# The sample part of a width-31 depthwise convolution: one product of four samples and one sum over the taps, in place of 31 taps of 64 columns

## What is computed

```
u  = glu[..., :512] * sigmoid(glu[..., 512:])
cv = causal_dwconv(conv_hist, u, w_dw)          # width 31, each channel by itself
cv = silu(layer_norm(cv + b_dw, ln_conv_g, ln_conv_b))
br_a = cv @ w_conv_out
```

## Time and profile before

| | |
|---|---|
| time, median of 3 runs | 1377.58 us (1369.18 to 1380.51) |
| profiled execution, first to last instruction | 1365.4 us |
| the same execution's own time beside the span | not recorded; the fastest of the runs shown is 3.8 us above this span, the median 12.2 us |
| busy: PE, DVE, ACT, POOL | 1240.6, 730.9, 410.0, 419.1 us |
| mean granted PE clock | 0.950 |

### The profile page before, as it was taken

How to read it: one execution, slowest core, us unless ns; L and a number is a source line. 1 busy time by engine, 2 the same in 40 slices (tenths; PEclk the granted TensorE clock), 3 DMA queues, 4 the chain that set the end, 5 groups by cost and what they waited for, 6 DMA issues and landing times.

```text
span 1365.4 us, 21526 instructions
## 1 busy us (share of the span) xinstructions
PE 1240.6 (91%) x8681; PEld 1158.4 (85%) x8681; DVE 730.9 (54%) x1147; ACT 410.0 (30%) x675; POOL 419.1 (31%) x193
## 2 busy tenths in 40 slices
PE   6987898887899889999889999968999999999993
PEld 6985787887899679999889654967999999999992
DVE  4785555998899673468750241688211211211257
ACT  4335110212222343223552321236312312312312
POOL 3331213102111114334554100346333333333332
PEclk9998787999899979999999999989999999999996
DMA  6111202010100503232454434111222222222201
GB/s 219 63 61 51 93 32 93 17 31 32 47 32 32 56 6 117 77 109 77 132 193 172 166 123 154 62 62 33 92 78 79 91 78 79 90 77 81 90 32 69
DMA packets 37480, 111.98 MB, mean 82 GB/s; under 512 B 12192, under 2 KB 12704, under 8 KB 34976
## 3 DMA queue, kind: packets, MB, share of 16 engines
q1 hardware_dynamic: 31520, 105.77, 22.9%
q10 hardware_dynamic: 5888, 5.18, 2.0%
HBM read 103.40 MB, written 7.53 MB: 81 GB/s over the span
## 4 chain that ended last, share of the span: by engine, by line
PE 66%; DVE 13%; issue 2%; ACT 2%; ACTq 0%; DVEq 0%
PE bank L374 50%; PE bank L582 5%; PE bank L758 4%; DVE cv L1241 2%; PE bank L385 1%; DVE res L1690 1%; PE bank L706 1%; PE bank L722 1%; DVE res L1688 1%; DVE lns L1677 1%; PE bank L742 1%; DVE h_lo L1683 0%; PE bank L468 0%; DVE lns L1531 0%; PE bank L636 0%
## 5 line engine op out<-in xcount | busy, mean ns | idle before, releaser
L338 POOL TENSOR_TENSOR w_lo<-w_raw,w_hi 128x1024 fp32r<-128x1024 f32 x152 | 385.7, 2540 | 862.4 <-ACT w_hi L842 862.4
L842 ACT ACTIVATE w_hi<-w_raw 128x1024 fp32r<-128x1024 f32 x152 | 160.5, 1057 | 271.9 <-PE bank L374 230.2
L374 PE MATMUL bank<-x_hi,w_hi 128*128 128x288 f32 x640 | 202.1, 316 | 16.4 <-DVE x_lo L1224 8.3
L374 PE MATMUL bank<-x_lo,w_hi 128*128 128x288 f32 x640 | 194.9, 305 | 0.0
L374 PE MATMUL bank<-x_hi,w_lo 128*128 128x288 f32 x640 | 194.2, 303 | 0.0
L374 PE MATMUL bank<-h_hi,w_hi 128*128 128x288 f32 x608 | 180.1, 296 | 2.2 <-ACT ht L1192 1.7
L374 PE MATMUL bank<-h_lo,w_hi 128*128 128x288 f32 x608 | 179.4, 295 | 0.0
L374 PE MATMUL bank<-h_hi,w_lo 128*128 128x288 f32 x608 | 178.7, 294 | 0.0
L374 PE MATMUL bank<-hid_hi,w_hi 128*128 128x288 f32 x496 | 146.8, 296 | 0.0
L374 PE MATMUL bank<-hid_lo,w_hi 128*128 128x288 f32 x496 | 146.3, 295 | 0.0
L374 PE MATMUL bank<-hid_hi,w_lo 128*128 128x288 f32 x496 | 145.8, 294 | 0.0
(11 more groups left out here) (347 smaller groups left out, 2363.6 us busy)
## 6 DMA issues: line engine op xcount, KB each, us to landing
w_raw<-w SPq DMA_DIRECT2D x152, 512.0 KB, 3.3
kv<-kT SPq DMA_DIRECT2D x8, 1024.0 KB, 5.4
kv<-v SPq DMA_DIRECT2D x8, 1024.0 KB, 4.8
xraw<-xT SPq DMA_DIRECT2D x4, 576.0 KB, 6.2
yT<-res SPq DMA_DIRECT2D x8, 288.0 KB, 2.2
sst<-sdelta SPq DMA_DIRECT2D x4, 512.0 KB, 6.4
sdelta_out<-sst ACTq DMA_DIRECT2D x4, 512.0 KB, 2.6
memraw<-memT SPq DMA_DIRECT2D x1, 1024.0 KB, 4.7
```

The source lines that it names most:

```text
L338: nc.gpsimd.tensor_tensor(wlo[:, s], raw[:, s % RAW], whi[:, s].bitcast(f32), sub)\
L374: ins = nc.tensor.matmul(bank[:, 0:b - a], lhsT=w[:, slot, kb], rhs=m[:, kb, a:b], start=(opens and i == 0 and j == 0), stop=(closes and i ...
L842: A_(whi[:, c % RING], raw[:, c % RAW], ACT.Copy).then_inc(hi_ready, 1)
```

## The change

The wide taps stay, one instruction each, but each now waits for the tap before it (`chc.wait()`). The 31 sample taps of a block become two entries, one for each four samples: a product of all 4 x 8 x 31 windows with the 31 weights into a scratch tile `taps31` (128 x 992), and a sum over the last dimension into the 32 columns of cv. A block has 33 entries instead of 31 pairs, and a sample entry counts as three taps in its slot. The slot after L1505 takes two taps instead of one. The bias of the sample columns is added at the end for all four blocks in one instruction, and after it an empty instruction counts `cv_ready`, on which ACT's squares now wait.

```diff
+    taps31 = at("taps31", R1 + 13.5, [P, DEC_BATCH // 2, DEC_SEQ, CONV_K])
...
-        act.wait_ge(S("cv_taps"), 2 * CT * CONV_K)
+        act.wait_ge(S("cv_ready"), 1)
...
-        todo = [(j, k) for j in range(CT) for k in range(CONV_K)]
+        todo = [(j, k) for j in range(CT) for k in range(CONV_K + 2)]
+
+        def wide_tap(j, k):
+
+            w, dst = pc("w_dw", j * CONV_K + k), cv[:, j, PT]
+            if k == 0:
+                return V.tensor_scalar(dst, u[:, j, 0:SEQ], w, pc("b_dw", j), mul, add)
+            return V.scalar_tensor_tensor(dst, u[:, j, k:k + SEQ], w, dst, mul, add)
+
+        def wide_samples(j, i):
+
+            n = DEC_BATCH // 2
+            first = u[:, j, UP + i * n * US:UP + (i + 1) * n * US]
+            rows = bass.AP(first.tensor, first.offset, [first.ap[0], (US, n), (1, DEC_SEQ), (1, CONV_K)])
+            w = par[:, PAR["w_dw"] + j * CONV_K:PAR["w_dw"] + (j + 1) * CONV_K]
+            chc(V.tensor_tensor(taps31[:], rows, w.unsqueeze(1).unsqueeze(1).broadcast_to([P, n, DEC_SEQ, CONV_K]), mul))
+            chc.step(V.tensor_reduce(tiled(cv[:, j, ST], DEC_SEQ)[:, i * n:(i + 1) * n], taps31[:], X, add))
 
         def wide_taps(n, blocks):
 
-            while n and todo and todo[0][0] < blocks:
+            while n > 0 and todo and todo[0][0] < blocks:
                 j, k = todo.pop(0)
-                conv_taps(chc, lambda kk: pc("w_dw", j * CONV_K + kk), lambda kk: u[:, j, kk:kk + SEQ],
-                          lambda kk: u_s(j)[:, :, kk:kk + DEC_SEQ], cv[:, j, PT], tiled(cv[:, j, ST], DEC_SEQ), [k],
-                          bias=pc("b_dw", j))
-                n -= 1
+                chc.wait()
+                if k < CONV_K:
+                    chc.step(wide_tap(j, k))
+                    n -= 1
+                else:
+                    wide_samples(j, k - CONV_K)
+                    n -= 3
...
-                between(1, 1)
+                between()
...
-        wide_taps(len(todo), CT)
+        wide_taps(3 * len(todo), CT)
         chc.wait()
+        ch(V.tensor_tensor(cv[:, :, ST], cv[:, :, ST], bc(par[:, PAR["b_dw"]:PAR["b_dw"] + CT], SAMPLE), add))
+        V.engine_nop().then_inc(S("cv_ready"), 1)
```

## The result

| | before | after |
|---|---|---|
| median of 19 runs each, in turn on one chip | 1370.32 us (1363.85 to 1380.51) | 1376.88 us (1373.27 to 1386.15) |
| profiled execution, span | 1365.4 us | 1373.9 us (its own time 1375.72) |
| busy: PE, DVE | 1240.6, 730.9 us | 1247.4, 727.9 us |
| mean granted PE clock of that execution | 0.950 | 0.939 |

The ratio is 1.005, with a 95% interval of 1.003 to 1.0069: the change costs 4 to 9 us. The range 1374 to 1398 holds the time, and the rise that I worked out, 7.4 us, is near the 6.6 measured. But the predicted 1385 is 8 us too high: it lies 14.7 us above the kernel before, more than twice what the change costs. And "a measurement here tells about 1% from no change" was wrong: 19 runs of each tell 0.2%, so what I called no change is a small loss that can be seen.

The account below looks back on a forecast made before the run. It took TensorE's 28.4 us of waits for VectorE, and the fixed tap slots, as the limits; -3.0 gains, +2.9 slot losses, +6.5 end, +1.0 clock gave +7.4 us, forecast 1385 us on the three-run median, range 1374 to 1398.

Parts of the forecast that it names:

- The end: After the last tile's L1505: five leftover tap entries and the bias delay the first channel sum, +6.5 us, nothing covering it.
- The slots: Tap slots in front of TensorE's gaps: gains of 3.0 us from cheaper taps, losses of 2.9 us, cancelling.
- Block 0's first half: Block 0's first sample product and sum, behind six taps before an L1465 gap, lengthen it by 0.9 us.
- block 1's product beside POOL: Block 1's first half, in the slot at 337.87 with its POOL wait, on the longest L1505 gap: +1.4 us.
- the second L1436 gap: Grows by 0.3 us, because a stopped wide tap needs 0.6 us after POOL where a sample tap needs 0.1.
- Prices: VectorE instruction costs: product 1.18 us, sum 1.17 us, half a channel block 2.4 us, wide taps starting 0.78 us apart.
- half rate: Rival: overlapping windows or sums over 31 run at half rate, 4.9 us a half, +22 us, 1400 us; chance 0.17.
- stops vanish: Rival: taps in front of six gaps no longer stop for POOL, about -7 us, 1371 us; chance 0.09.
- end hidden: Rival: VectorE runs ahead or TensorE has other work, so only the bias stays exposed, 1378 us; chance 0.14.
- the sum: Whole kernel: -3.0 + 2.9 + 6.5 + 1.0 = +7.4 us, span 1365.4 to 1372.8, or 1385 on the median of three runs.
- My slot arithmetic: VectorE's undisturbed total for the convolution taps: 107 us before, 109 after, so it hardly moves.
- 1 us for the clock: Behind the longer end standstill, a longer stretch of low granted clock: 1 us, bounds nothing and 3 us.

Follow-up runs that it names:

- run 1: Changed kernel with the slot after the sample step su taking 13 taps instead of 2, so taps finish before the last tile: 1373.08 us, ratio 1.0012.
- run 2: Changed kernel with the slot after L1525 (L1505 before) back to one tap, leaving more taps for the end: 1383.35 us, ratio 1.0089.
- run 3: Kernel before, pairs kept, with every tap waiting for the tap just before it: 1391.35 us, ratio 1.0148.
- run 4: Changed kernel without the sample products and sums, sample columns getting only their bias: 1367.64 us, ratio 0.9958.
- run 9: Changed kernel with a lighter slot table, fewer taps in the first pair of heads, more in the second: 1355.60 us, ratio 0.9859.
- run 11: Repeat of the changed kernel with the lighter slot table (fewer taps in the first pair of heads): 1350.31 us, ratio 0.9810.
- run 6: Kernel before, sample taps kept, with a slot table that moves taps into the sample phase: 1366.66 us, ratio 0.9939.
- run 7: Changed kernel with the sample-phase slot table, plus wide taps of channel blocks 1 and 2 taken in turn: 1355.06 us, ratio 0.9846.
- run 8: Kernel before, pairs kept, with a lighter slot table, fewer taps in the first pair of heads, more in the second: 1356.57 us, ratio 0.9853.
- run 10: Repeat of the kernel before with the lighter slot table (fewer taps in the first pair of heads): 1352.54 us, ratio 0.9803.
- run 5: Changed kernel with a slot table that moves taps into the sample phase and leaves none for the last tile: 1361.15 us, ratio 0.9891.
- run 12: Changed kernel with the lighter slot table, plus wide taps of channel blocks 1 and 2 taken in turn: 1353.55 us, ratio 0.9825.

## Where the prediction held, and where it failed

**The end** was worked out row by row and came so. L1529 was to start at 456.31 and did. VectorE was to be free at 456.83, the tap to be held until 458.65 (459.15), the first half done at 461.0 (461.6), the last at 463.9 (464.4), the bias at 464.4 (464.9). Predicted standstill 9 to 10 us, measured 9.11; the term 6.5, measured 6.0. Runs 1 and 2 move the standstill both ways.

**The slots** were to cancel, −3.0 and +2.9, and nearly did: TensorE's waits from 250 to 450 us come to 21.1 us before and to 21.2 after, both without the first 0.92, and in front of them some 1 us was won. In front of L519 the first gap went from 3.27 to 2.87 us (−0.4; the two together 0.7, predicted 0.6). Block 0's first half lengthened its gap from 1.86 to 3.36 (+1.5, predicted +0.9); block 1's product beside POOL took 3.21 us in place of 1.19 and its gap went from 3.38 to 4.94 (+1.6, predicted +1.4). L1472 stayed at 2.94. The gain at L1436's gap (0.4) can be read only where the clock is alike: run 2, the same program up to there, has 4.91 against 5.31. One sign was wrong: the second L1436 gap was to grow by 0.3 and fell from 2.35 to 1.31, because POOL's product came later (355.98, before 352.11) and stopped the taps at 357.95 for 0.6 us, where before it had been 2.1.

**Prices.** Product 1.19 and sum 1.19 us where nothing stops them (1.18 and 1.17 predicted), two taps in 1.53 us, so 0.78 apart. This refutes *half rate*. In the timeline after, taps still stop beside POOL's products (2.32 us at 456.83): *stops vanish* is refuted, and *end hidden* by the 9.11. What the empty engine instruction was to cost, nothing, fits: the bias ends at 464.89 and the first channel sum starts at 464.93.

**What failed: the base of the sum.** I added +7.4 us to the median of the three runs shown, 1377.58, although the sum was made against a span of 1365.4. Over 19 runs that median is 1370.32, 7 us less, so the forecast stood 14.7 us above the kernel that it was a change to, where 6.6 were measured; on 1370.32 the same sum gives 1377.7. An execution's own time is its span + 1.8 us (1373.9 and 1375.72 after), so the sum against its own time gives 1365.4 + 1.8 + 7.4 = 1374.6, 2.3 below the measured median. Three runs that spread over 11 us could not carry the base. The same spread misled me on the resolution: I gave 0.77 to a time that could not be told from no change, and the interval, 0.3 to 0.7%, leaves no change out.

**A figure that contradicted my own text.** VectorE's busy time was to fall by 15 to 30 us and fell by 3.0. I took row sums: those of the taps fell from 146.5 to 131.9 us. But a sample tap's 400 ns overlapped its neighbours, and the engine's busy time counts such time once. My slot arithmetic (107 to 109 us of occupied time) had said that it would hardly move.

**A term that was missing: the clock ahead of the block phase.** The sum has 1 us for the clock, behind the standstill. In the profile after, TensorE's clock was at half for all of 200 to 236 us, and not before (last section). From the L519 gap to the block phase the profile after takes 81.4 us, the one before 77.4, and run 2, the same program up to there without that stretch, 76.1. So the profiles put 5 us of clock into this comparison. By the rows without it, that part is 1.3 us shorter and the block phase 4.8 longer than before: 3.5 us, where the sum without its clock term had 6.4. That 7.4 came so near to 6.6 is therefore in part luck.

**What stays open** is how much of the 6.6 us is clock, and why. Of the executions of the kernel before that were timed beside runs 1 to 4, 20 of 26 had a mean clock of 0.945 or more (beside the later runs 8 of 14, 7 of 11 and 3 of 11); of the 19 after, 1. At a like mean clock the two kernels differ less: at 0.943 to 0.945 nine of before have a median of 1374.87 us and five of after 1376.88; at 0.938 to 0.941 five of before have 1378.43 and nine of after 1376.72. A standstill at the lower level itself takes down the mean, so this does not settle the share. Whether the change itself makes the low clock more frequent was not tried.

## What to carry to other kernels

Count where the work stands, not how much it is: eight products and sums or 120 small taps were the same to within what 12 runs tell, while the slot tables brought both 15 to 28 us below the kernel before. Work that is dealt out in fixed slots should be done before the last slot: here TensorE had nothing else to do for whatever was left there. Add a predicted difference to the execution from which its rows come, and take three runs for no more than their spread.

## What the runs showed of the hardware

**The granted clock splits one program's executions.** TensorE's row for 200 to 236 us (stretch, PE busy, PEld, DVE, ACT, POOL, clock, DMA), before, after, run 9 and run 11:

```profile
200.00:236.00 36.00, 30.02 (x193) 28.00 (x192) 20.94 (x29) 3.62 (x5) 10.50 (x6) 0.85 0.21 78
```

```profile
200.00:236.00 36.00, 36.00 (x150) 33.85 (x151) 14.21 (x16) 1.44 (x2) 10.34 (x5) 0.50 0.16 60
```

```profile
200.00:236.00 36.00, 36.00 (x166) 34.12 (x166) 19.36 (x21) 1.88 (x4) 6.91 (x5) 0.55 0.09 36
```

```profile
200.00:236.00 36.00, 31.45 (x196) 29.75 (x196) 25.07 (x33) 4.34 (x7) 10.32 (x5) 0.82 0.24 88
```

Runs 9 and 11 are one program. In 9 TensorE was busy all 36 us at a mean of 0.55 of full speed, so nearly throughout at the level of 1.2 GHz (after at 0.50, throughout); in 11 it was mostly at 2.4. It did not stand still before it fell: in the profile after, the clock was 1.00 and TensorE busy 9.00 of 9 us from 190 to 199. Their timelines at the entry of the phase and at the start of the block phase, 9 and then 11:

```profile
177.99 0.68 PE L519 MATMUL bank<-sw 64*64 64x64 f32 x8 [2.20 <-DVE sw L1411]
...
253.89 0.66 PE L583 MATMUL bank<-cst,qkv 128*128 128x128 f32 x4 [0.92 <-DVE dl L1477]
```

```profile
174.42 0.68 PE L519 MATMUL bank<-sw 64*64 64x64 f32 x8 [2.21 <-DVE sw L1411]
...
241.51 0.66 PE L583 MATMUL bank<-cst,qkv 128*128 128x128 f32 x4 [0.92 <-DVE dl L1477]
```

75.9 against 67.1 us: 8.8 us, and the clock is the one difference that I see. The low stretch is not tied to the products: of the 14 profiles those after and of runs 1, 4 and 6 to 10 have it (0.50 to 0.56, TensorE busy 36.00 of 36 us), among them three of the kernel before with other slots; those before and of runs 2, 3, 5, 11 and 12 do not (0.74 to 0.85). The block phases behind them are alike (199.6 and 200.7 us), and the spans are 1362.4 and 1348.0. What decides between the two was not found. Within each kernel the mean clock goes with the time: over runs 9 and 11 the six executions at 0.953 and above took 1347.6 to 1353.1 us, the six at 0.948 and below 1354.3 to 1364.1.

**The clock behind the standstill.** Busy times and clock behind the standstill before the row sums; after, then before, then run 2:

```profile
462.00:472.00 10.00, 4.50 (x10) 1.11 (x11) 7.27 (x10) 5.98 (x9) 0.00 (x0) 0.50 0.80 65
```

```profile
461.00:464.00 3.00, 2.69 (x6) 0.51 (x5) 1.51 (x2) 1.45 (x3) 0.00 (x0) 0.50 1.50 148
464.00:474.00 10.00, 10.00 (x61) 7.21 (x60) 4.60 (x7) 2.06 (x2) 0.00 (x0) 0.99 1.11 29
```

```profile
461.00:477.50 16.50, 3.84 (x8) 0.90 (x9) 14.15 (x17) 5.99 (x9) 0.00 (x0) 0.50 0.42 38
```

After 9.11 us of standstill the clock is at the lower level for 10 us, after 3.10 for 3, after 16.67 for 16.5. In run 2 most of it lies in the standstill itself, where it costs nothing; after, about half. But in run 9 the mean is 0.52 over 450 to 460 us behind only 3.32, so the length of the standstill alone does not set it. The 1 us that I took for this could not be told from the rest.
